# Half-wise norms: the second half's column sums closed on VectorE straight behind the last residual, ahead of the first half's second chunk

## The chip, the cores and the metric

The kernel runs on one core of a Trainium2 chip. The metric is the device time of one execution in microseconds (us); lower is better. Several runs of one kernel are given by their median. A profile shows one further execution: its span is counted from the first to the last instruction.

## The reference

The program computes two transformer blocks one after the other on 512 tokens with 1024 features, in float32. The first block has a recurrent mixer layer (HGRN2 and retention heads) and a sparse-attention layer, each followed by a SwiGLU feed-forward part and with RMS norms. The second block has an attention layer and a convolution layer, each followed by an MLP with a squared ReLU, modulated by a condition vector. What the change touches are the norms at five places: the final RMS norm of the first block and the four layer norms of the second.

```python
def rms_norm(x, g):
    xf = x.astype(jnp.float32)
    return (xf * lax.rsqrt(jnp.mean(xf * xf, axis=-1, keepdims=True) + EPS) * g).astype(x.dtype)

def layer_norm(x, g, b):
    xf = x.astype(jnp.float32)
    mu = jnp.mean(xf, axis=-1, keepdims=True)
    var = jnp.mean(jnp.square(xf - mu), axis=-1, keepdims=True)
    return ((xf - mu) * lax.rsqrt(var + EPS) * g + b).astype(x.dtype)
...
        x = layer_norm(DEEPNORM_ALPHA * x + g1 * y, ln_g[l, 0], ln_b[l, 0])
        h = modulate(x, sh2, sc2)
        x = layer_norm(DEEPNORM_ALPHA * x + g2 * sq_relu_mlp(h, mlp_w1[l], mlp_w2[l]), ln_g[l, 1], ln_b[l, 1])
```

## The kernel before

**Layout.** Features lie on the 128 partitions: the residual x is 8 tiles of 128 features by 512 tokens. Every product is made in three matmuls, because each operand is split into a high part (rounded, made by ScalarE) and a low part (the difference, made by VectorE, and in the norms by GpSimd): high by high, high by low, low by high. Weights stream in units of 128x1024, two to a pair, through `w_raw`, `w_hi` and `w_lo`. TensorE (PE) works through these units from start to end, and the other engines prepare what it reads. Every engine's order of instructions is written out by hand, and counting semaphores tie them together; an engine takes its instructions strictly in the order written.

**The five half-wise norms.** Five products end in a norm whose result the next product reads: `ffn1_down2` (called with r = 4, an RMS norm, the start of the attention stage behind it), `out2` (r = 5), `mlp0_down3` (r = 6), `out3` (r = 7) and `mlp1_down3` (r = 8, the end of the program). On each engine the end of such a product stands in a function `close_halves`, and the start of the product behind it in `open_halves`. They split the 512 tokens into two halves of 256 columns. TensorE finishes features 6 and 7 (slots s = 0 and 1) for half 0, then for half 1, so that the norm of half 0 proceeds while TensorE still multiplies for half 1.

**What the norm does, by name.** On VectorE:
- `take(half, s)` adds a finished product to x (L2063 for r = 4, L2065 else) and, for r > 4, subtracts a rough mean into `norm_xc` (L2071).
- `close(half)` adds the last tile to the sums over features: L2083 adds the last `norm_xc` tile to s1 (r > 4 only), and L2087 adds the last square to s2. GpSimd has made the sums up to there (L523, L529); ScalarE makes the squares (`square`, L1123).
- `variance(half)` (L2096 to L2099, r > 4), then ScalarE's root (L1134), then `scale(half)`: the reciprocal (L2105) and a diagonal matrix `norm_diag` (L2108).
- `centre(half, c)` (L2120, r > 4) and `normal(half, c)` (L2129 for r = 4, L2133 else) make chunk c of a half, two features of eight. There are four chunks to a half.

On TensorE `sum_half(r, half)` sums s1 and s2 over partitions (L2483 for the mean, L2477 for the columns of sums) and `spread_half` spreads the scale over partitions (L2492). On ScalarE `chunk(half, c)` modulates a chunk (L1144, two instructions) and rounds it to `h_hi` (L1152; in the last norm L1148 writes x instead). GpSimd's `low_halves` makes `h_lo` from both (L538). The next product's matmuls (L2467) wait for each chunk's `h_lo`.

The orders around the change are these. ScalarE:

```python
square(1, 0)
...
chunk(0, 0)
square(1, 1)
...
chunk(0, 1)
...
chunk(0, 2)
root_half(1)
```

TensorE's `open_halves` begins with `sum_half(r, 1)`, then multiplies chunk 0 for both slots and chunk 1 for slot 0, then does `spread_half(r, 1)`, then the rest of half 0 (five groups of six matmuls), then half 1, chunk by chunk, twelve matmuls each.

Of the kernel before, what the change touches and what calls it, by code (L numbers as in the profile page):

```python
# [171 lines left out]
def program(nc, dram, out):  # L172
    with ExitStack() as ctx:
# [242 lines left out]
        def half_cols(half):  # L416
            return slice(T // 2 * half, T // 2 * half + T // 2)

        def half_count(r, half):

            return 2 * r - 3 + half

        def halves_before(r, half, step):

            return step * (2 * (r - 4) + half)

        def centred_before(r, half, step):

            return step * (2 * (r - 5) + half)

        def stat_half(half):
            return psum[2 + 4 * half]
# [958 lines left out]
        def _(dve):  # L1391
# [631 lines left out]
            def gated_residual(name, part, r=None):  # L2023

                def body(i, s, m):
                    dve.wait_ge(unit_done, 2 * i + s + 1)
                    xm = x[:, bass.ds(m, 1), :]
                    dve.scalar_tensor_tensor(xm, row(psum[s]), mod[:, bass.ds(8 * part + m, 1), 0], xm,  # L2028
                                             ALU.mult, ALU.add).then_inc(bank_free[s], 1)
                    if r:  # L2030
                        dve.wait_ge(bank_free[s], i + 1)
                        dve.wait_ge(shift_done, r - 4)
                        dve.scalar_tensor_tensor(N["xc"][:, bass.ds(m, 1), :], row(psum[3]), -1.0 / P, xm,  # L2033
                                                 ALU.mult, ALU.add).then_inc(xc_done, 1)
                if r:
                    pairs(name, body, 0, PAIRS[name] - 2)
                    close_halves(name, part, r, body)
                else:
                    pairs(name, body)
                    dve.wait_ge(bank_free[1], PAIR0[name] + PAIRS[name])  # L2040

            def close_halves(name, part, r, body):
# [4 lines left out]
                def take(half, s):  # L2047

                    cols, m = half_cols(half), 6 + s
                    xm = x[:, m, cols]  # L2050
                    if half == 0:
                        dve.wait_ge(unit_half, 2 * (r - 4) + s + 1)
                        if r == 4:
                            ins = dve.tensor_tensor(xm, xm, psum[s][:, cols], ALU.add)
                        else:
                            ins = dve.scalar_tensor_tensor(xm, psum[s][:, cols], mod[:, 8 * part + m, 0:1], xm, ALU.mult,
                                                           ALU.add)
                        ins.then_inc(bank_free[s], 1)
                        dve.wait_ge(bank_free[s], i + 1)
                    else:  # L2060
                        dve.wait_ge(unit_done, 2 * i + s + 1)
                        if r == 4:
                            ins = dve.tensor_tensor(xm, xm, psum[6 + s][:, cols], ALU.add)  # L2063
                        else:
                            ins = dve.scalar_tensor_tensor(xm, psum[6 + s][:, cols], mod[:, 8 * part + m, 0:1], xm,  # L2065
                                                           ALU.mult, ALU.add)
                        ins.then_inc(x_half, 1)
                        dve.wait_ge(x_half, 2 * (r - 4) + s + 1)
                    if r == 4:
                        return  # L2070
                    dve.scalar_tensor_tensor(N["xc"][:, m, cols], psum[3][:, cols], -1.0 / P, xm, ALU.mult, ALU.add)\  # L2071
                       .then_inc(xc_half, 1)

                def close(half):

                    cols, last = half_cols(half), KT - 1
                    if r == 4:
                        dve.wait_ge(acc_done, 5 + half)
                    else:
                        acc = 6 + centred_before(r, half, 2)  # L2080
                        dve.wait_ge(acc_done, acc + 1)
                        dve.wait_ge(xc_half, centred_before(r, half, 2) + 2)
                        dve.tensor_tensor(N["s1"][:, cols], N["s1"][:, cols], N["xc"][:, last, cols], ALU.add)\  # L2083
                           .then_inc(s1_done, 1)
                        dve.wait_ge(acc_done, acc + 2)
                    dve.wait_ge(sq_half, halves_before(r, half, 2) + 2)
                    dve.tensor_tensor(N["s2"][:, cols], N["s2"][:, cols], N["sq"][:, last, cols], ALU.add)\  # L2087
                       .then_inc(s2_done, 1)
# [21 lines left out]
                def both(ap):  # L2110
                    return row(ap[:, 0:T // 2]).broadcast_to([P, 2, T // 2])

                def centre(half, c):

                    if r == 4:
                        return
                    if c == 0:
                        dve.wait_ge(mean_done, centred_before(r, half, 1) + 1)
                    xc = N["xc"][:, 2 * c:2 * c + 2, half_cols(half)]
                    dve.scalar_tensor_tensor(xc, both(mean_half(half)), -1.0 / D, xc, ALU.mult, ALU.add)\  # L2120
                       .then_inc(centred, 1)

                def normal(half, c):

                    if c == 0:
                        dve.wait_ge(scale_done, half_count(r, half))
                    cols, two = half_cols(half), slice(2 * c, 2 * c + 2)
                    if r == 4:
                        dve.tensor_tensor(N["xc"][:, two, cols], x[:, two, cols], both(stat_half(half)), ALU.mult)\  # L2129
                           .then_inc(y_done, 1)  # L2130
                        return
                    dve.wait_ge(centred, centred_before(r, half, 4) + c + 1)
                    dve.tensor_tensor(N["y"][:, two, cols], N["xc"][:, two, cols], both(stat_half(half)), ALU.mult)\  # L2133
                       .then_inc(y_done, 1)
# [18 lines left out]
                normal(0, 0)  # L2153
                centre(0, 1)
                take(1, 1)
                normal(0, 1)
                close(1)
                centre(0, 2)
                normal(0, 2)
                variance(1)  # L2160
# [14 lines left out]

            pairs("ffn1_down2", add_residual, 0, 2)
            close_halves("ffn1_down2", None, 4, add_residual)
            dve.wait_ge(ctx_in, 16)
            for k in range(KT):
# [975 lines left out]
```

## Time and profile before

| | us |
|---|---|
| median of 3 runs | 2628.8 |
| lowest and highest | 2627.44 and 2631.59 |
| the profiled execution's own time | 2632.85 |
| its span | 2631.0 |

In that span TensorE is busy for 2562.0 us, VectorE for 1581.0, ScalarE for 1048.3 and GpSimd for 258.3. Since TensorE is nearly always busy, what a local change is worth is read at the places where TensorE stands still. A row of the timeline gives the start in us, the duration in us, the engine, the line of the kernel, the operation, what it writes and reads, the shape, how many instructions are merged in the row, and in brackets how long the engine was idle before and who released it. An instruction's duration includes the time that it is held up after its start.

### The profile page before, as it was taken

How to read it: one execution, taken by the hardware profiler on the slowest of the kernel's cores; microseconds unless marked ns; L12 is line 12 of the kernel's file. 1: busy time of each engine (PE TensorE's matmuls, PEld its weight loads, DVE VectorE, ACT ScalarE, POOL GpSimd, SP SyncE). 2: the span in 40 equal slices, each digit the busy share in tenths (PEclk: the TensorE clock that was granted, in tenths of full speed). 3: DMA queues.
4: the chain of work that ended last, by engine and by line, in shares of the span. 5: the costliest groups of instructions: out<-in, count | busy, mean ns of one | idle time of the engine just before them, and what ended most of it. 6: DMA issues, size and time to landing. Idle time of an engine off the chain costs nothing.

```text
span 2631.0 us, 37917 instructions
## 1 busy us (share of the span) xinstructions
PE 2562.0 (97%) x13134; PEld 2109.1 (80%) x13134; DVE 1581.0 (60%) x2460; ACT 1048.3 (40%) x1663; POOL 258.3 (10%) x187
## 2 busy tenths in 40 slices
PE   8999999999999999999989999999999999999997
PEld 6887788888887878888878776788888888888886
DVE  6764665656578866565665786555555665644445
ACT  5334522223357852222353266553223422522333
POOL 2320100000320010000030100310000401300002
PEclk9999999999999999999999999999999999999999
DMA  3221344444320034444432100234444243332322
GB/s 133 73 88 65 119 137 144 144 145 149 135 73 26 26 112 143 144 143 144 144 120 72 41 1 1 80 112 144 144 144 143 95 145 114 104 102 96 96 96 80
DMA packets 79338, 277.48 MB, mean 105 GB/s; under 512 B 8448, under 2 KB 11904, under 8 KB 78720
## 3 DMA queue, kind: packets, MB, share of 16 engines
q1 hardware_dynamic: 58560, 205.55, 23.9%
q10 hardware_dynamic: 20672, 70.51, 8.2%
q8 instruction: 68, 1.11, 0.2%
q14 instruction: 38, 0.31, 0.0%
HBM read 273.92 MB, written 2.10 MB: 105 GB/s over the span
## 4 chain that ended last, share of the span: by engine, by line
PE 86%; DVE 7%; ACT 3%; issue 1%; DMA 1%; POOL 1%; ACTq 0%; DVEq 0%; SPq 0%; POOLq 0%
PE banks L2423 64%; PE banks L2564 5%; PE banks L2993 2%; PE banks L2467 2%; PE banks L2829 2%; DVE w_lo L1403 1%; PE banks L2935 1%; PE banks L2867 1%; PE banks L2844 1%; PE banks L2598 1%; DMA w_raw<-weights 1%; PE banks L2947 1%; ACT w_hi L679 1%; PE banks L2964 1%; DVE ada_raw L1426 0%
## 5 line engine op out<-in xcount | busy, mean ns | idle before, releaser
L679 ACT ACTIVATE w_hi<-w_raw 128x1024 fp32r<-128x1024 f32 x367 | 386.4, 1053 | 621.7 <-PE banks L2423 515.1
L2423 PE MATMUL banks<-h_hi,w_hi 128*128 128x512 f32 x1600 | 628.0, 392 | 1.1 <-DVE w_lo L1403 0.7
L2423 PE MATMUL banks<-h_hi,w_lo 128*128 128x512 f32 x1600 | 623.1, 389 | 0.0
L2423 PE MATMUL banks<-h_lo,w_hi 128*128 128x512 f32 x1600 | 622.9, 389 | 0.0
L1403 DVE TENSOR_TENSOR w_lo<-w_raw,w_hi 128x1024 fp32r<-128x1024 f32 x367 | 474.1, 1292 | 108.7 <-ACT w_hi L679 91.9
L2423 PE MATMUL banks<-g_hi,w_hi 128*128 128x512 f32 (+1 forms) x1108 | 427.5, 386 | 9.9 <-DVE w_lo L1403 8.8
L2423 PE MATMUL banks<-g_hi,w_lo 128*128 128x512 f32 (+1 forms) x1108 | 423.6, 382 | 0.0
L2423 PE MATMUL banks<-g_lo,w_hi 128*128 128x512 f32 (+1 forms) x1108 | 423.6, 382 | 0.0
L2423 PEld LDWEIGHTS banks<-h_hi,w_hi 128*128 128x128 f32 x1600 | 300.4, 188 | 66.8 <-issue 2.8
L2423 PEld LDWEIGHTS banks<-h_lo,w_hi 128*128 128x128 f32 x1600 | 300.5, 188 | 62.7 <-issue 1.7
L2423 PEld LDWEIGHTS banks<-h_hi,w_lo 128*128 128x128 f32 x1600 | 300.4, 188 | 62.8
L2423 PEld LDWEIGHTS banks<-g_hi,w_hi 128*128 128x128 f32 x1108 | 208.7, 188 | 58.8 <-DVE w_lo L1403 14.8
L2423 PEld LDWEIGHTS banks<-g_lo,w_hi 128*128 128x128 f32 x1108 | 208.8, 188 | 40.6 <-issue 1.0
L2423 PEld LDWEIGHTS banks<-g_hi,w_lo 128*128 128x128 f32 x1108 | 208.6, 188 | 40.5
L2028 DVE SCALAR_TENSOR_TENSOR x<-banks,mod,x 128x512 f32 (+1 forms) x72 | 53.9, 749 | 163.4 <-PE banks L2423 163.2
L1426 DVE CUSTOM_DVE_ANT_0 ada_raw<-ada_raw,rows_c 128x1024 f32<-128x1024 f32 x112 | 138.6, 1238 | 0.0
L2336 DVE TENSOR_TENSOR ffn_hid<-ffn_act 128x512 f32<-128x512 f32 x64 | 44.3, 692 | 131.9 <-ACT ffn_act L1347 131.9
L2564 PE MATMUL banks<-h_hi,w_hi 128*128 128x512 f32 x256 | 104.5, 408 | 10.3 <-DVE w_lo L1403 10.3
L1347 ACT ACTIVATE ffn_act<-banks 128x512 f32<-128x512 f32 x64 | 38.3, 598 | 189.1 <-PE banks L2423 184.2
L523 POOL TENSOR_TENSOR norm_s<-norm_xc 128x512 f32<-128x512 f32 x4 | 8.8, 2198 | 952.6 <-DVE norm_xc L2033 952.6
L2564 PE MATMUL banks<-h_hi,w_lo 128*128 128x512 f32 x256 | 101.1, 395 | 0.0
L2564 PE MATMUL banks<-h_lo,w_hi 128*128 128x512 f32 x256 | 101.1, 395 | 0.0
(409 smaller groups left out, 3304.5 us busy)
## 6 DMA issues: line engine op xcount, KB each, us to landing
w_raw<-weights SPq DMA_DIRECT2D x384, 512.0 KB, 3.3
ada_raw<-ada ACTq DMA_DIRECT2D x112, 512.0 KB, 3.3
nsa_bias<-nsa_bias ACTq DMA_DIRECT2D x6, 512.0 KB, 3.7
x<-x SPq DMA_DIRECT2D x4, 512.0 KB, 6.9
out<-x SPq DMA_DIRECT2D x8, 256.0 KB, 2.1
mix_cum<-ret_tab ACTq DMA_DIRECT2D x1, 1024.0 KB, 4.8
rows_c<-c_rows ACTq DMA_DIRECT2D x1, 1024.0 KB, 5.5
nsa_w<-cmp_w ACTq DMA_DIRECT2D x1, 1024.0 KB, 5.5
```

The lines of the kernel that those rows point to most:

```text
L679: act.activation(w_hi[s][:], w_raw[s][:], ACT.Copy).then_inc(w_hi_done, 1)
L1347: act.activation(F["act"][:, s, :], psum[s], ACT.Relu).then_inc(bank_free[s], 1)
L1403: dve.tensor_tensor(w_lo[s][:], w_raw[s][:], w_hi[s][:].bitcast(F32), ALU.subtract)\
L1426: dve.tensor_tensor_reduce(ada_raw[:], ada_raw[:], c_row[:, who, :], 1.0, 0.0, ALU.mult, ALU.add, ada_col[:]).then_inc(ada_done, 1)
L2028: dve.scalar_tensor_tensor(xm, row(psum[s]), mod[:, bass.ds(8 * part + m, 1), 0], xm, ALU.mult, ALU.add).then_inc(bank_free[s], 1)
L2336: dve.tensor_tensor(F["hid"][:, s, :], F["act"][:, s, :], F["act"][:, s, :], ALU.mult)\
L2423: mm = pe.matmul(bank, w[s][:, k, :], m[:, k, :], start=(n == 0 and a == 0), stop=(n == kts - 1 and a == 2))
L2467: mm = pe.matmul(bank[:, cols], w[slot][:, k, :], m[:, k, cols], start=(k == 0 and a == 0), stop=(k == kts - 1 and a == 2))
L2564: mm = pe.matmul(bank, w[s][:, k, :], m[:, k, :], start=(k == 0 and a == 0), stop=(k == KT - 1 and a == 2))
L2598: mm = pe.matmul(grams[:, cols(t)], left[:, h, cols(t)], right[:, h, cols(t)], start=True, stop=True)
L2829: mm = pe.matmul(banks[:, 4 - 2 * (j % 2) + b, 0:W], S["qs"][:, h, qi * P:(qi + 1) * P], S["ks"][:, b, part, m // 4, 0:W], start=(part == ...
L2993: mm = pe.matmul(banks[:, 2 + 2 * b + a, 0:c1 - c0], q, keys[:, c0:c1], start=True, stop=True)
```

## The change

In VectorE's `close_halves`, the call `close(1)` moves up by one line: from behind `normal(0, 1)` to ahead of it. It holds for all five norms.

```diff
@@ -2153,8 +2153,8 @@
                 normal(0, 0)
                 centre(0, 1)
                 take(1, 1)
+                close(1)
                 normal(0, 1)
-                close(1)
                 centre(0, 2)
                 normal(0, 2)
                 variance(1)
```

On VectorE, at the end of `ffn1_down2` (r = 4), the order changes as follows; `norm_s_68` is s2, `norm_xc` is where this norm puts its normalized chunk, and a row that ends in x2 or x3 stands for as many equal instructions.

```order
 L2063 TENSOR_TENSOR x<-x,banks 128x256 [waits unit_done]
-L2129 TENSOR_TENSOR norm_xc<-x,banks 128x2x256 [waits x_half]
-L2087 TENSOR_TENSOR norm_s_68<-norm_s_68,norm_sq 128x256 [waits sq_half,acc_done]
-L2129 TENSOR_TENSOR norm_xc<-x,banks 128x2x256 x2
+L2087 TENSOR_TENSOR norm_s_68<-norm_s_68,norm_sq 128x256 [waits sq_half,acc_done,x_half]
+L2129 TENSOR_TENSOR norm_xc<-x,banks 128x2x256 x3
 L2105 RECIPROCAL norm_r<-norm_r 128x2 [waits root_done]
```

The one sum, which waits for ScalarE's square (`sq_half`), now stands ahead of the chunk that filled that wait.

On VectorE, at the end of `out2` (r = 5), the order changes as follows, and in the same way for r = 6, 7 and 8; `norm_s_73` is s1.

```order
 L2065 SCALAR_TENSOR_TENSOR x<-banks,mod,x 128x256 [waits unit_done]
 L2071 SCALAR_TENSOR_TENSOR norm_xc<-banks,x 128x256 [waits x_half]
-L2133 TENSOR_TENSOR norm_y<-norm_xc,banks 128x2x256 [waits centred]
 L2083 TENSOR_TENSOR norm_s_73<-norm_s_73,norm_xc 128x256 [waits xc_half,acc_done]
 L2087 TENSOR_TENSOR norm_s_68<-norm_s_68,norm_sq 128x256 [waits sq_half,acc_done]
+L2133 TENSOR_TENSOR norm_y<-norm_xc,banks 128x2x256 [waits centred]
 L2120 SCALAR_TENSOR_TENSOR norm_xc<-banks,norm_xc 128x2x256
 L2133 TENSOR_TENSOR norm_y<-norm_xc,banks 128x2x256 [waits centred]
```

The first L2133 row, chunk 1 of half 0, goes behind the two sums. No instruction is added or removed, and the other engines' orders stay as they are.

## Rows read from the trace of the kernel before

**Rows 1.** Page, part 1: busy us (share of the span) and instructions.

```profile
PE 2562.0 (97%) x13134; PEld 2109.1 (80%) x13134; DVE 1581.0 (60%) x2460; ACT 1048.3 (40%) x1663; POOL 258.3 (10%) x187
```

**Rows 2.** Waits of PE, 2060 to 2130 (around r = 6): total us, times, longest us.

```profile
PE banks L2483 <- DVE norm_s L2083: 3.2, 2, 2.9
PE banks L2467 <- POOL h_lo L538: 1.1, 2, 0.8
```

**Rows 3.** Timeline around the sums of half 1 in out2, all engines.

```profile
1705.07 0.42 DVE L2071 SCALAR_TENSOR_TENSOR norm_xc<-banks,x 128x256 f32<-128x256 f32 x1
1705.41 0.68 DVE L2133 TENSOR_TENSOR norm_y<-norm_xc,banks 128x512 f32<-128x512 f32 x1
1705.58 0.40 ACT L1123 ACTIVATE norm_sq<-norm_xc 128x256 f32<-128x256 f32 x1
1705.75 1.26 POOL L538 TENSOR_TENSOR h_lo<-norm_sq,h_hi 128x512 fp32r<-128x512 f32 x1 [1.05 <-ACT h_hi L1152]
1706.00 1.29 DVE L2083 TENSOR_TENSOR norm_s<-norm_s,norm_xc 128x256 f32<-128x256 f32 x1
1707.21 0.41 DVE L2087 TENSOR_TENSOR norm_s<-norm_s,norm_sq 128x256 f32<-128x256 f32 x1
1707.44 0.67 PE L2483 MATMUL banks<-norm_s,tab 128*128 128x256 f32 x2 [2.93 <-DVE norm_s L2083]
1707.55 0.68 DVE L2120 SCALAR_TENSOR_TENSOR norm_xc<-banks,norm_xc 128x512 f32<-128x512 f32 x1
1708.26 0.69 DVE L2133 TENSOR_TENSOR norm_y<-norm_xc,banks 128x512 f32<-128x512 f32 x1
1708.99 1.09 ACT L1144 ACTIVATE norm_sq<-norm_y,aux,ln_cols 128x256 f32<-128x256 f32 x2 [1.11 <-DVE norm_y L2133]
```

**Rows 4.** Timeline of out2 further on: root, diagonal, spread, chunks of half 1.

```profile
1710.65 0.28 ACT L1134 ACTIVATE norm_r<-norm_st,tab 128x2 f32<-128x2 f32 x1
1711.16 1.22 DVE L2108 TENSOR_TENSOR norm_diag<-tab,norm_r 128x256 f32<-128x256 f32 x1
1712.49 0.64 PE L2492 MATMUL banks<-norm_diag,tab 128*128 128x256 f32 x2
1713.17 0.69 DVE L2133 TENSOR_TENSOR norm_y<-norm_xc,banks 128x512 f32<-128x512 f32 x1 [0.19 <-PE banks L2492]
1717.51 0.39 PE L2467 MATMUL banks<-h_hi,w_hi 128*128 128x256 f32 x1 [0.82 <-POOL h_lo L538]
```

**Rows 5.** Timeline of ffn1_down2 (r = 4), the same place.

```profile
1349.39 0.40 ACT L1123 ACTIVATE norm_sq<-x 128x256 f32<-128x256 f32 x1
1349.56 1.27 POOL L538 TENSOR_TENSOR h_lo<-norm_sq,h_hi 128x512 fp32r<-128x512 f32 x1 [3.23 <-ACT h_hi L1152]
1349.89 1.22 DVE L2087 TENSOR_TENSOR norm_s<-norm_s,norm_sq 128x256 f32<-128x256 f32 x1 [0.63 <-ACT norm_sq L1123]
1351.74 1.09 ACT L1144 ACTIVATE norm_sq<-norm_xc,mod,ln_cols 128x256 f32<-128x256 f32 x2 [0.30 <-DVE norm_xc L2129]
1353.88 1.26 DVE L2108 TENSOR_TENSOR norm_diag<-tab,norm_r 128x256 f32<-128x256 f32 x1
1356.09 1.05 PE L2492 MATMUL banks<-norm_diag,tab 128*128 128x256 f32 x2
```

**Rows 6.** Timeline of mlp1_down3 (r = 8), the same place.

```profile
2616.17 0.68 DVE L2133 TENSOR_TENSOR norm_y<-norm_xc,banks 128x512 f32<-128x512 f32 x1
2616.29 0.42 ACT L1123 ACTIVATE norm_sq<-norm_xc 128x256 f32<-128x256 f32 x1 [1.88 <-DVE norm_xc L2071]
2616.76 0.42 DVE L2083 TENSOR_TENSOR norm_s<-norm_s,norm_xc 128x256 f32<-128x256 f32 x1
2617.43 0.68 DVE L2120 SCALAR_TENSOR_TENSOR norm_xc<-banks,norm_xc 128x512 f32<-128x512 f32 x1
```

**Rows 7.** Windows of PE in out2: us, busy us (matmuls), granted clock, DMA.

```profile
1709.00:1712.00 3.00, 3.00 (x16) 0.50 0.00 0
1713.00:1716.00 3.00, 3.00 (x27) 1.00 0.00 0
```

## The prediction

> **What bounds the kernel now.** I read the page's busy times first, then TensorE's waits, then the timeline of each of the five norms. The reader should see three things. TensorE is busy for 97% of the span [rows 1], so a local change counts only where TensorE stands still or where its matmuls wait for a chunk. Behind `out2` it stands still twice: 2.93 us until the sum L2483, released by VectorE's L2083, and later 0.82 us for GpSimd's `h_lo` [rows 3, 4]. The waits around r = 6 show the same two [rows 2] (3.2 us in two waits, since the first half's sum waits a little too), and the view reads alike for r = 7, so one reading serves three norms. The long wait invites the change, since s1 and s2 come sooner if they stand further up. But a wait that is shortened is worth something only if the same engine does not wait later for something that has not moved.
>
> So I followed the 0.82 us back. The matmuls of half 1 wait for `h_lo` of half 1, chunk 0. That comes from `normal(1, 0)` at 1713.17, which stands behind the spread (1712.49) and the diagonal (1711.16), behind the root at 1710.65 [rows 4]. ScalarE does the root only after chunk (0, 2), which began at 1708.99 after ScalarE had been idle for 1.11 us until VectorE's L2133 of 1708.26 [rows 3]. From a chunk's start to the root is 1710.65 - 1708.99 = 1.66 us, and that is what one ScalarE chunk costs. The sums are in this chain only because chunk 2 stands behind them on VectorE. What counts is when VectorE gives ScalarE chunks 1 and 2, not when the sums are done.
>
> **The change, part by part.** It adds and removes nothing, and no DMA moves. L2083 and L2087 go ahead of one L2133, in r = 4 only L2087. Queued behind them on VectorE are now chunks 1 and 2 of half 0, and ScalarE waits for these.
>
> *r = 5, 6, 7.* Before: L2133 starts at 1705.41, ScalarE takes chunk 1 right behind its 0.68 us, and VectorE's L2083 is held up meanwhile: it takes 1.29 us [rows 3] where the same instruction takes 0.42 with GpSimd quiet [rows 6]. GpSimd's `h_lo` ran from 1705.75 to 1707.01, and VectorE's next instruction starts at 1707.21, 0.20 after that end.
> After: L2071 ends at 1705.49. A wait for another instruction's end costs about 0.1 (in r = 4 the square ends at 1349.79 and L2087 starts at 1349.89 [rows 5]), so L2083 runs from 1705.60 to 1706.02. That is before GpSimd's `h_lo` asks (1705.75), so GpSimd goes second: about 1705.9 to 1707.2. L2087 needs ScalarE's square, which ends at 1705.98, and the same 0.1: ready at 1706.08. By then GpSimd is at work, and L2087 is held until 1707.2, the next instruction starting 0.20 later, at 1707.4. Only now L2133 for chunk 1 runs, 0.69, to 1708.09; ScalarE starts chunk 1 0.04 later, at 1708.13, instead of at about 1706.13. Chunk 2 follows 1.66 later, at 1709.79 instead of 1708.99, since ScalarE's idle 1.11 us absorbed the rest. The root, the diagonal, the spread and all of half 1 are 0.80 later. The diagonal keeps its long 1.22 us [rows 4], a hold-up like L2083's, since it and the `h_lo` that holds it both hang on chunk 2. TensorE's gain, s1 sooner by 1.4 us and s2 by 0.1, ends in a longer wait for the spread. The cost is 0.80 each, 2.40 in all.
>
> The bounds for one of these norms: if L2087 slips in before GpSimd, VectorE goes on at 1706.08 + 0.34 = 1706.42 (0.34 is from L2087's start to the next instruction's, 1707.21 to 1707.55) and chunk 2 starts 0.98 earlier than above, a gain of 0.18. If L2083 too is caught by GpSimd, it ends as before and L2087 ends at 1707.62, so L2133 starts at 1707.55: a loss of 0.95. I take 0.80, since the VectorE sums and diagonals of this size that meet a GpSimd instruction (1.29, 1.22, 1.22, 1.26) all show a full hold-up [rows 3 to 5].
>
> The Trainium skill, "SBUF — State Buffer", section "SBUF: two separate sides", says that an instruction of VectorE with two SBUF inputs and one of GpSimd exclude each other for the whole instruction. [...]
>
> *r = 4.* L2087 has no use for its new place: it waited 0.63 us for ScalarE's square already and started at 1349.89 [rows 5]. The square stands behind ScalarE's chunk 0, which doesn't move. So the sum comes no earlier, while chunk 1 comes behind L2087, held by GpSimd (1.22 us): L2129 starts 0.20 behind GpSimd's end of 1350.83, at 1351.03, ScalarE has chunk 1 at 1351.03 + 0.69 + 0.04 = 1351.76 and chunk 2 at 1353.42 instead of 1351.74, so the root and the diagonal are 1.68 later. The diagonal ended at 1355.14 and now ends at 1356.82. TensorE did not need it before 1356.09 [rows 5]; it now waits until about 1356.9. Slack of 0.95 is eaten, and 0.8 is left as a loss.
>
> *r = 8.* ScalarE makes no `h_lo` input here and GpSimd is quiet, so nothing is held. But two waits are now uncovered. Before, L2133 filled them and L2120 started at 2617.43. After, the square ends at 2616.71 and L2087 starts at 2616.81; L2133 follows 0.34 later and L2120 another 0.59 behind it (as L2083 behind L2133, 2616.17 to 2616.76), at 2617.74 [rows 6]. That is 0.3 later, and all behind it is VectorE's own chain. The bounds are 0, if some of it is made up by a wait for TensorE's sums that comes sooner, and 0.5.
>
> The sum: 3 x 0.80 + 0.8 + 0.3 = 3.5 us. Against the profiled execution (2632.85, span 2631.0) that gives 2636.4. That execution lies 4.05 above the median of the runs, so the forecast for a median is 2628.8 + 3.5 = 2632.3 us.
>
> **The rivals.** *Clock.* After the 2.93 us of idleness TensorE falls to its lower level, 1.2 GHz, from 1709 to 1712 at least (14 matmuls start in 3 us, 0.214 each), and is back at 2.4 GHz from 1713 on (25 start in 3 us, 0.12 each) [rows 7]; their counts hold two begun before. It comes back just before the spread, which took 0.64; in r = 4 it took 1.05 [rows 4, 5]. The new order cuts one long idle time into several: until s1, until s2, for chunk 1's `h_lo` (about 0.6 us) and for the spread (up to 1.2 us). If the clock is still low at the spread, 0.4 to 0.5 comes on top, and if it stays low into half 1, twelve matmuls of a chunk take 12 x 0.214 = 2.57 us against ScalarE's pitch of 1.66, 0.9 more per chunk. With one such chunk and the spread in each of four norms that is 4 x 1.4 = 5.6 more: 2637.9. It decides from the point where the lower level lasts beyond the spread. For it speaks that the low level lasted 3 us and more although TensorE multiplied without a break; against it, that the first idle time is shorter than before. It is slower by over 0.2%.
> *The sums slip through.* L2087 runs before GpSimd in r = 5 to 7 (the bound above): -3 x 0.18 + 0.8 + 0.3 = +0.6, 2629.4. Against it: GpSimd has been waiting since 1705.75, ahead of L2087's 1706.08.
> *TensorE decides after all.* With s1 at 1706.0 the clock may never fall, and the 14 matmuls of [rows 7] would take 0.12 us each instead of 0.214: 1.3 us per norm, 2628.8 - 3.9 + 1.1 = 2626.0, or less with the few low ones outside that window. It needs TensorE to be what ends the stage; the 0.82 us for `h_lo` speaks against it. The Trainium skill, "TensorE: Matmul & The Clock Gate", section "Why this matters for your kernels", advises against idle gaps between bursts of matmuls, because the clock then drops; by that advice a shorter gap is a gain, and the rows agree only as far as the clock itself goes.
> That the change would not do what it says is the case in r = 4, and is in the forecast.
>
> **How the numbers follow.** A measurement of this kernel can tell about 0.2%, 5.3 us, from no change. Forecast 0.60 (of itself 2.5 to 5 us more, nearly all within 0.2%), clock 0.24, slipping through 0.10, TensorE decides 0.06. Faster by over 0.2%: 0.03, half of the last. Slower by over 0.2%: 0.20 from the clock and 0.04 from the forecast's upper edge, 0.24. Within: the remaining 0.73. The range reaches from below the slipping case to the clock case: 2628.0 to 2637.5.
>
> **What would show it.** In the new profile L2083 in `out2` should take about 0.42 and start 0.1 behind L2071; L2087 should be the long one (about 1.2 us), in r = 4 as before; ScalarE's idle time should stand before chunk 1 and not before chunk 2; the root should come 5.96 us after L2071's end instead of 5.16; TensorE's 2.93 us should become about 1.5 and a new wait should stand at L2492. The forecast is wrong if the end of half 1's chunks, counted from L2071, comes no later than before, if L2492 is reached without a wait, or if the clock stays low in half 1.

## The result, and the profile after

The changed kernel took 2634.62 us (median of 14 runs, 2631.74 to 2638.57) against 2627.99 us for the kernel before (14 runs, 2624.25 to 2635.58): a ratio of 1.0021, with a 95% interval of 1.0013 to 1.0028. By the ratio that is 5.5 us slower, between 3.4 and 7.4; the two medians alone lie 6.6 us apart. The forecast was 3.5 us more, or 2632.3 us, so the direction held, the time lies in the range of 2628.0 to 2637.5, and the size was at the interval's lower end. The profiled execution has a span of 2636.8 us, 5.8 more than before.

TensorE's waits around r = 6, which answer to [rows 2] (total us, times, longest us):

```profile
PE banks L2483 <- DVE norm_s L2083: 1.9, 2, 1.7
PE banks L2467 <- POOL h_lo L538: 1.8, 2, 1.6
PE banks L2492 <- DVE norm_diag L2108: 1.0, 1, 1.0
PE banks L2477 <- DVE norm_s L2087: 0.3, 1, 0.3
```

The long wait for s1 fell from 2.93 to 1.66 us. In its place stand a wait for s2 (0.3), one for chunk 1's `h_lo` (1.6) and one for the diagonal (1.0). Two kinds of wait have become four, and together they are longer (5.0 us against 4.3). In `out2` TensorE waits only for s1 (1.66), s2 (0.31) and the diagonal (0.28) and is never idle behind the spread: its matmuls run at the lower clock from 1709.3 to 1719.5 there and arrive later.

The timeline of `out2` in the changed kernel answers to [rows 3] and [rows 4]. The columns are as there.

```profile
1707.30 0.42 DVE L2071 SCALAR_TENSOR_TENSOR norm_xc<-banks,x 128x256 f32<-128x256 f32 x1
1707.81 0.40 ACT L1123 ACTIVATE norm_sq<-norm_xc 128x256 f32<-128x256 f32 x1
1707.83 0.43 DVE L2083 TENSOR_TENSOR norm_s<-norm_s,norm_xc 128x256 f32<-128x256 f32 x1
1707.98 1.40 POOL L538 TENSOR_TENSOR h_lo<-norm_sq,h_hi 128x512 fp32r<-128x512 f32 x1 [1.05 <-ACT h_hi L1152]
1708.32 1.35 DVE L2087 TENSOR_TENSOR norm_s<-norm_s,norm_sq 128x256 f32<-128x256 f32 x1
1708.40 0.67 PE L2483 MATMUL banks<-norm_s,tab 128*128 128x256 f32 x2 [1.66 <-DVE norm_s L2083]
1709.59 0.68 DVE L2133 TENSOR_TENSOR norm_y<-norm_xc,banks 128x512 f32<-128x512 f32 x1
1710.30 1.10 ACT L1144 ACTIVATE norm_sq<-norm_y,aux,ln_cols 128x256 f32<-128x256 f32 x2 [2.09 <-DVE norm_y L2133]
...
1713.61 0.28 ACT L1134 ACTIVATE norm_r<-norm_st,tab 128x2 f32<-128x2 f32 x1
1714.12 1.23 DVE L2108 TENSOR_TENSOR norm_diag<-tab,norm_r 128x256 f32<-128x256 f32 x1
1715.41 1.22 PE L2492 MATMUL banks<-norm_diag,tab 128*128 128x256 f32 x2 [0.28 <-DVE norm_diag L2108]
```

L2083 is short now (0.43) and L2087 is the one that GpSimd holds (1.35). ScalarE stands idle for 2.09 us ahead of chunk 1, where it stood 1.11 ahead of chunk 2. The root comes 5.89 us behind the end of the last residual (1707.72), where it was 5.16. The spread takes 1.22 us where it took 0.64, since TensorE is at its lower clock (1.2 GHz). The window row of TensorE (us, busy us, granted clock, DMA share, GB/s) answers to [rows 7]:

```profile
1713.00:1716.00 3.00, 2.72 (x11) 0.50 0.00 0
```

In this table each mark is counted from the end of the last residual (L2071, for r = 4 L2063), in us. The last column is the end of the last matmul of half 1, the moment from which TensorE runs on without the norm.

| norm | root before | root after | spread takes, before | after | half 1 ends, before | after |
|---|---|---|---|---|---|---|
| r = 4 | 4.86 | 6.49 | 1.05 | 1.22 | 19.18 | 20.07 |
| r = 5 | 5.16 | 5.89 | 0.64 | 1.22 | 18.69 | 19.97 |
| r = 6 | 5.16 | 5.88 | 0.65 | 1.22 | 18.71 | 19.94 |
| r = 7 | 5.16 | 5.88 | 0.65 | 0.70 | 18.72 | 19.41 |
| r = 8 | 3.30 | 3.60 | 1.22 | 1.22 | (VectorE's chain) | +0.30 |

The differences are 0.89, 1.28, 1.23, 0.69 and 0.30: 4.4 us. The rest of the 5.8 us between the two spans lies where nothing was altered: 0.3 before the first of these norms and 1.0 between r = 4 and r = 5. Of that 1.0, 0.8 arises between 1496 and 1521, where the lower clock lasted longer: from 1500 to 1512 TensorE's mean granted clock was 0.57, and 0.72 before.

### The profile page after: what moved, and what is told of

Same layout as the page of the kernel before. It is cut to its first block, busy times and chain, and to the rows that moved or that the text cites. A ratio compares the mean times of both kernels' runs of the same rounds, so it can differ in the third digit from the quotient of the medians.

```text
span 2636.8 us, 37917 instructions
## 1 busy us (share of the span) xinstructions
PE 2567.9 (97%) x13134; PEld 2113.2 (80%) x13134; DVE 1582.2 (60%) x2460; ACT 1047.6 (40%) x1663; POOL 258.6 (10%) x187
## 3 DMA queue, kind: packets, MB, share of 16 engines
q8 instruction: 68, 1.11, 0.2%
## 4 chain that ended last, share of the span: by engine, by line
PE 86%; DVE 7%; ACT 4%; issue 1%; DMA 1%; POOL 1%; ACTq 0%; DVEq 0%; SPq 0%; POOLq 0%
PE banks L2423 64%; PE banks L2564 5%; PE banks L2993 3%; PE banks L2467 2%; PE banks L2829 2%; DVE w_lo L1403 1%; PE banks L2935 1%; PE banks L2867 1%; PE banks L2844 1%; PE banks L2598 1%; DMA w_raw<-weights 1%; ACT w_hi L679 1%; PE banks L2947 1%; PE banks L2964 1%; ACT norm_sq L1144 0%
```

## The experiments

**Three questions.** Is the loss made by the order, that is, by L2087 held by GpSimd ahead of ScalarE's chunks? What is the clock's part? And why is the measured loss above the forecast? In what follows "residual" stands for the end of the last L2071 (L2063 for r = 4), from which marks are counted.

**The hold-up alone.** GpSimd's first `h_lo` waits until s2 is closed; the order on VectorE is the changed one.

```diff
                         pool.wait_ge(y_hi, 4 * KT + halves_before(r, half, 4) + c + 1)
+                        if half == 0 and c == 0:
+                            pool.wait_ge(s2_done, half_count(r, 1))
```

> The changed kernel, but GpSimd starts the first h_lo of half 0 only when VectorE has closed s2, so that L2087 meets no GpSimd instruction (r = 4 to 7). Order theory with the hold-up as its cause: L2087 takes 0.42 instead of 1.35, chunk 2 on ScalarE starts 3.3 to 3.4 us behind the residual in r = 5 to 7 (changed kernel 4.24, before 3.50) and about 4.1 in r = 4 (4.84, before 3.20); half 1 ends at 18.5 to 18.7 in r = 5 to 7, about 19.4 in r = 4. Total against before -0.3 to +0.6 us, ratio 0.9999 to 1.0002. Rival (the order costs even without the hold-up, or the late h_lo of chunk 0 costs as much): the ratio stays at 1.0015 to 1.002.

Measured: ratio 0.9997 (0.9988 to 1.0006). The timeline in `out2` (this kernel's lines are shifted by two: L2085 and L2089 are the sums, L2135 is chunk 1, L540 `h_lo`):

```profile
1702.20 0.42 DVE L2085 TENSOR_TENSOR norm_s<-norm_s,norm_xc 128x256 f32<-128x256 f32 x1
1702.68 0.43 DVE L2089 TENSOR_TENSOR norm_s<-norm_s,norm_sq 128x256 f32<-128x256 f32 x1
1703.02 0.68 DVE L2135 TENSOR_TENSOR norm_y<-norm_xc,banks 128x512 f32<-128x512 f32 x1
1703.25 1.27 POOL L540 TENSOR_TENSOR h_lo<-norm_sq,h_hi 128x512 fp32r<-128x512 f32 x1 [1.94 <-DVE norm_s L2089]
1703.73 1.09 ACT L1146 ACTIVATE norm_sq<-norm_y,aux,ln_cols 128x256 f32<-128x256 f32 x2 [1.16 <-DVE norm_y L2135]
```

With GpSimd out of the way L2089 takes 0.43 us, ScalarE waits 1.16 instead of 2.09, the root stands at 4.95 and half 1 ends at 18.49, 18.49 and 18.50 in r = 5 to 7, 0.2 below the kernel before. The order by itself costs nothing there. What costs is one instruction of VectorE held for 0.93 us ahead of the chunks. The rival, a loss without the hold-up, falls in these three norms. In r = 4 it does not. Counted from L2087's start (the next run shows why), half 1 of r = 4 ended at 17.41, against 18.18 with the hold-up and 16.58 to 16.73 in the order of before, all with the clock high at the spread. So there the hold-up is half of the loss. The other half stays when GpSimd is out of the way, and chunk 1 then stands behind a sum that itself waits 0.86 us for its square. The expectation of 19.4 for r = 4 was 1.1 too high: ScalarE stood 0.5 earlier relative to the residual, and the clock was high. In r = 8, where GpSimd is quiet, the 0.30 stayed.

**Only r = 4 changed.**

```diff
                 take(1, 1)
+                if r == 4:
+                    close(1)
                 normal(0, 1)
-                close(1)
+                if r > 4:
+                    close(1)
```

> The sums move ahead only in r = 4; r = 5 to 8 keep the order of before. Order theory: in r = 4 chunk 2 on ScalarE starts 4.8 us behind the end of the last residual (before 3.20), TensorE waits about 0.9 us for the spread and the last matmul of half 1 ends 20.0 +- 0.1 behind the residual (before 19.2); r = 5 to 7 end at 18.7 and r = 8 has its root at 3.30, as before. Total +0.8 to +0.9 us. Rival (the clock alone makes the loss): r = 4 ends at 19.2 to 19.4 wherever TensorE's level is the same as before, whatever ScalarE's chunks do.

One run, 2631.45 us, which says nothing of so small a difference, and its profile: half 1 of r = 4 ended at 20.19 and chunk 2 started at 4.97. TensorE waited 0.27 us ahead of the spread, not the 0.9 expected. The last residual came 0.15 earlier relative to ScalarE here, so I count r = 4 from L2087's start, which ScalarE's square sets in every version: before 17.83, the changed kernel 18.71, this one 18.69. The clock is low at the spread in all three, so the loss of 0.88 is the order's: the spread starts 0.73 later in the changed kernel and 0.72 here, and takes 1.22 us instead of 1.05 now that TensorE stands idle ahead of it. r = 6, 7 and 8 were as before, but r = 5, whose order is that of before, ended at 19.97 instead of 18.69. Its sums ran at the lower clock (L2486 and L2480 are the sums there, L2495 the spread):

```profile
1704.74 1.19 PE L2486 MATMUL banks<-norm_s,tab 128*128 128x256 f32 x2 [2.93 <-DVE norm_s L2083]
1705.72 1.71 PE L2480 MATMUL banks<-tab,norm_s 128*128 128x1 f32 x8
1709.65 0.42 DVE L2108 TENSOR_TENSOR norm_diag<-tab,norm_r 128x256 f32<-128x256 f32 x1
1711.11 0.60 PE L2495 MATMUL banks<-norm_diag,tab 128*128 128x256 f32 x2
```

They took 1.19 and 1.71 us where they took 0.67 and 0.95 before (granted clock 0.50 from 1704.7 to 1707.5; 1.00 at the same place before). The variance and the diagonal came later too, but they did not set the end: the diagonal was done at 1710.07, and TensorE, busy without a pause since its sums, reached the spread only at 1711.11. Here TensorE decided, and an unaltered norm lost 1.3 us. So where the low clock falls in a norm is worth as much as the change, and it is not fixed by the program. A single profile can't price a norm without a look at its clock.

**The changed kernel again**, unaltered.

> The changed kernel once more, unaltered. In its first profile half 1 ended 20.0, 19.9 and 19.4 us behind the last residual in r = 5, 6, 7, with the spread at 1.22, 1.22 and 0.70. Order theory: the marks of ScalarE and VectorE repeat within 0.05 (chunk 2 at 4.24, root at 5.88), and each of r = 5 to 7 ends at 19.4 where the spread takes 0.70 and at 19.9 to 20.0 where it takes 1.22; which of them has which is free to differ from the first profile. Ratio 1.0013 to 1.0028. Rival (the low clock belongs to a place in the program): the same two norms have 1.22 again.

Measured: 2637.27 us (9 runs), ratio 1.0024 (1.0014 to 1.0034). Half 1 ended at 19.95, 19.94 and 19.43 in r = 5 to 7, chunk 2 started at 4.23 or 4.24 and the root stood at 5.88 or 5.89: VectorE's and ScalarE's marks repeat within 0.02. r = 5 and 6 had the spread at 1.22 again and r = 7 at 0.70, as the rival had said, so two profiles can't tell a place in the program from chance. r = 4 differed: its spread took 0.70.

```profile
1347.53 1.19 DVE L2087 TENSOR_TENSOR norm_s<-norm_s,norm_sq 128x256 f32<-128x256 f32 x1 [0.90 <-ACT norm_sq L1123]
1354.44 0.70 PE L2492 MATMUL banks<-norm_diag,tab 128*128 128x256 f32 x2 [0.89 <-DVE norm_diag L2108]
```

**The changed kernel with the clock held up.** Filler matmuls go into a bank that nothing reads, 6 ahead of half 1's sums and 4 ahead of its spread.

```diff
                 pe.wait_ge(w_lo_done, 2 * p0 + 1)
+                filler(6)
                 sum_half(r, 1)
...
                 steps(0, 0, 1)
+                filler(4)
                 spread_half(r, 1)
```

Each filler is `pe.matmul(psum[5], w_hi[1][:, 0, :], w_hi[1][:, 0:4, :]...)`, 512 columns.

> The changed kernel with filler matmuls (128x512, high part of a weight by itself, into a bank that nothing reads): 6 ahead of half 1's sums and 4 ahead of its spread, in TensorE's idle time there, for r = 4 to 7. Nothing else is altered. Theory (order 0.7 to 0.8 per norm plus 0.5 where the clock is low at the spread): the clock stays at its upper level, the spread takes 0.70 in every norm, half 1 ends at 19.4 in r = 5 to 7, ratio 1.0007 to 1.0015 of before. Rival (the order costs nothing and the clock all): ratio 0.999 to 1.0003.

Measured: ratio 1.0016 (1.0007 to 1.0025), the point a little above what was expected. The spread took 0.70 in all four norms, for example in `out2`:

```profile
1705.28 0.28 ACT L1134 ACTIVATE norm_r<-norm_st,tab 128x2 f32<-128x2 f32 x1
1705.94 1.08 PE L2527 MATMUL banks<-w_hi 128*128 128x512 f32 x4
1707.07 0.70 PE L2492 MATMUL banks<-norm_diag,tab 128*128 128x256 f32 x2
```

Half 1 ended at 19.44, 19.44 and 19.45. So with the clock up the order costs 0.7 per norm in r = 5 to 7, and the low clock at the spread adds the other 0.5 (1.22 - 0.70). By the marks the filler takes part of the loss back, not all; the time alone doesn't tell this version from the changed kernel (1.0016 against 1.0021 and 1.0024, with overlapping intervals). The rival, that the clock is everything, falls: its upper end of 1.0003 lies below the interval. Set beside the run without the hold-up, which had the same order and the spread at 0.70 or 0.71 in these norms too, half 1 ends 0.95 later, so the gain of that run was the hold-up's and not the clock's.

**The kernel before with the clock held up**: the same filler, 10 ahead of the sums, none ahead of the spread.

> The kernel before with 10 filler matmuls ahead of half 1's sums (about 2.2 of the 2.93 us in which TensorE is idle), r = 4 to 7. If ScalarE's and GpSimd's chunks decide the end of the norm, TensorE's matmuls start half 0 at the upper level and only wait longer: half 1 ends at 18.7 in r = 5 to 7 as before, up to 1 us less in r = 4 where the matmuls limit the spread; ratio 0.9995 to 1.0001. Rival (TensorE decides after all): each norm ends 1.3 us sooner, -4 to -5 us, ratio 0.998 to 0.9985.

Measured: ratio 0.9992 (0.9983 to 1.0001). The point lies below the expected 0.9995, and the interval touches the rival's 0.9985, so it is the marks that decide. Half 1 ended at 18.73, 18.73 and 18.72 in r = 5 to 7, within 0.04 of where the low clock had it. TensorE's matmuls of half 0 ran at 2.4 GHz, and it only waited longer, for the diagonal:

```profile
1703.31 0.70 PE L2483 MATMUL banks<-norm_s,tab 128*128 128x256 f32 x2 [0.59 <-DVE norm_s L2083]
1708.38 0.70 PE L2492 MATMUL banks<-norm_diag,tab 128*128 128x256 f32 x2 [1.35 <-DVE norm_diag L2108]
```

That refutes the third rival of the prediction for r = 5 to 7: a faster TensorE gains nothing there. But it has no slack to lose either. In the kernel before it reached the spread at 7.00 without a wait, 0.11 behind the end of the diagonal (6.89), and r = 5 of the run with only r = 4 changed shows that a slower TensorE costs 1.3. In r = 4 its speed does decide. Counted from L2087, half 1 ended at 17.83 before, with TensorE at its lower clock, and here at 16.60.

**s1 alone ahead** (r = 5 to 8), s2 behind chunk 1.

```diff
                 take(1, 1)
+                if r > 4:
+                    close(1, 1)
                 normal(0, 1)
-                close(1)
+                close(1, 2)
```

> Only L2083 (s1) goes ahead of chunk 1, for r = 5 to 8; L2087 (s2) stays behind chunk 1, and r = 4 is as before. Order theory: L2083 takes 0.42, no GpSimd in flight; chunk 1 is 0.5 later than before, L2087 is held by GpSimd and ends about 0.1 sooner, so chunk 2 starts 3.3 to 3.5 us behind the residual (before 3.50) and half 1 ends at 18.5 to 18.7: no loss, ratio 0.9995 to 1.0002 of before. Rival (any sum ahead of chunk 1 costs what it delays chunk 1): half 1 ends 0.4 to 0.5 later in three norms, +1.5 us, ratio 1.0006.

Measured: ratio 0.9997 (0.9989 to 1.0006). Chunk 2 started at 3.30 or 3.31 and half 1 ended at 18.51 and 18.50 in r = 5 and 6, and at 19.02 in r = 7, with the spread at 1.22. In `out2` (L2091 is s2, L2124 the centring of chunk 2):

```profile
1702.40 0.90 DVE L2091 TENSOR_TENSOR norm_s<-norm_s,norm_sq 128x256 f32<-128x256 f32 x1
1703.22 0.68 DVE L2124 SCALAR_TENSOR_TENSOR norm_xc<-banks,norm_xc 128x512 f32<-128x512 f32 x1
```

Half of what the change does is harmless: s1 meets no GpSimd instruction where it stands now. The loss is s2's. Behind chunk 1 it is held for a shorter time (0.90 us instead of 1.35), and most of that is covered by ScalarE's work on the chunk: ScalarE waits 0.38 us ahead of chunk 2.

**s2 in GpSimd's gap.** For r = 5 to 7, s1 ahead of chunk 1 and s2 behind the centring of chunk 2, when GpSimd has ended one `h_lo` and not begun the next.

```diff
                 take(1, 1)
+                if 4 < r < 8:
+                    close(1, 1)
                 normal(0, 1)
-                close(1)
-                centre(0, 2)
+                if 4 < r < 8:
+                    centre(0, 2)
+                    close(1, 2)
+                else:
+                    close(1)
+                    centre(0, 2)
```

> For r = 5 to 7 L2083 goes ahead of chunk 1 and L2087 behind the centring of chunk 2, in the gap between two of GpSimd's h_lo instructions; r = 4 and 8 as before. Order theory: L2087 takes 0.42 instead of 1.2 to 1.35, chunk 2 starts on ScalarE at 2.8 to 2.9 us behind the residual (before 3.50), root at 4.5 (before 5.16); the spread is then limited by TensorE's 18 low-clock matmuls, half 1 ends 0.3 to 0.7 sooner per norm, -0.9 to -2 us, ratio 0.9993 to 0.9997. Rival (the sums' own time decides): no gain, since s2 is not done sooner than before.

Measured: 2629.16 us against 2631.11 for the kernel before, measured beside it, ratio 0.9989 (0.998 to 0.9998): faster than the kernel before by an interval that just leaves out 1, and below the 0.9993 expected. In r = 6 (L2085 s1, L2137 chunk 1, L2124 the centring, L2091 s2, L2102 the subtraction in the variance):

```profile
2065.36 0.42 DVE L2085 TENSOR_TENSOR norm_s<-norm_s,norm_xc 128x256 f32<-128x256 f32 x1
2065.51 1.41 POOL L538 TENSOR_TENSOR h_lo<-norm_sq,h_hi 128x512 fp32r<-128x512 f32 x1 [1.04 <-ACT h_hi L1152]
2065.70 0.68 DVE L2137 TENSOR_TENSOR norm_y<-norm_xc,banks 128x512 f32<-128x512 f32 x1
2066.30 0.68 DVE L2124 SCALAR_TENSOR_TENSOR norm_xc<-banks,norm_xc 128x512 f32<-128x512 f32 x1
2066.90 0.42 DVE L2091 TENSOR_TENSOR norm_s<-norm_s,norm_sq 128x256 f32<-128x256 f32 x1
2068.41 1.15 DVE L2102 TENSOR_TENSOR norm_st<-norm_st 128x2 f32<-128x2 f32 x1
```

L2137 and L2124, which read one operand from PSUM, run at full speed while GpSimd works, and s2 takes 0.42. Half 1 ended at 18.15, 18.17 and 18.16, which is 0.55 sooner per norm, 1.6 us in all; the ratio's point says 2.9 and its interval 0.5 to 5.3. The rival, that only the moment of s2 counts, falls: s2 is closed at 2.07 behind the residual, hardly sooner than the 2.13 of before.

The last row shows what is still lost. The variance now comes so early that L2102, on 128x2 elements, meets GpSimd's next `h_lo` (2068.26 to 2069.55) and takes 1.15 us instead of 0.16. Chunk 3 queues behind it on VectorE, and the reciprocal behind chunk 3, so that the root, started at 4.54 and done at 4.84, is taken up only at 5.74. With s1 alone ahead the row before it was caught in the same way (0.92 us). In this version VectorE's own chain decides, not ScalarE's.

**The same with filler**, 6 ahead of the sums (r = 4 to 7) and 4 ahead of the spread (r = 5 to 7).

> The version with s1 ahead of chunk 1 and s2 in the gap of GpSimd (ratio 0.9989), with 6 filler matmuls ahead of half 1's sums and 4 ahead of the spread (none there in r = 4). Half 1 ended at 18.15 to 18.17 there with the spread at 0.70 in all three norms, so the filler has nothing to win in that state: 18.15 again, r = 4 up to 1 us less, ratio 0.9983 to 0.999. If filler delays the sums or the spread, half 1 ends later than 18.3.

Measured: ratio 0.999 (0.998 to 0.9999). Half 1 ended at 18.17 in all three norms, and r = 4 at 16.58 behind L2087 instead of 17.83. The filler gained nothing in r = 5 to 7 that the profile shows, and the two ratios don't tell the versions apart. Beside the kernel before with filler (18.73), which also has the clock high, the new order ends 0.56 sooner: the gain is the order's.

## Why the prediction was right, point by point

**Where the end of a norm is decided.** Right. ScalarE's chunks and the root behind them set it: the root moved by 0.73 and half 1 by 0.69 where the clock was the same (r = 7), and making TensorE faster in the kernel before moved nothing there. Two limits showed: TensorE stood level with the diagonal, so that a slower TensorE took over (19.97 in r = 5 of the run with only r = 4 changed), and in the versions with the two sums apart VectorE's chain did.

**The cost in r = 5 to 7**, forecast 0.80 each. The mechanism was right and the size a little high: L2083 started 0.11 behind L2071 and took 0.43, L2087 took 1.35, chunk 1 started at 2.58 (forecast 2.64), chunk 2 at 4.25 (4.30), the root at 5.89 (5.96). One reading of the rows was off: s1 comes 1.27 us sooner by them (1707.29 to 1706.02), not 1.4, and TensorE's wait became 1.66, not 1.5; nothing in the sum hangs on it. With the clock at its upper level at the spread the cost is 0.69 to 0.72. The bound "slips in before GpSimd" was what the run without the hold-up built, and its gain came out as 0.2 against the 0.18 worked out.

**The clock.** Given 0.24 as a rival, and at nothing in the sum; a part of it came. The spread took 1.22 instead of 0.64 in two norms of three, in both profiles of the changed kernel, which is 0.5 to 0.6 each. The larger part, twelve low matmuls of a chunk in half 1, did not: from the spread to the end of half 1 there was 12.28 us in r = 5, where the kernel before had 11.69, and the difference is the spread's own. The low level did last beyond the spread there, as the rival had asked (granted clock 0.50 from 1716.6 to 1719.5), but it fell on the rest of half 0. TensorE reached half 1 at 13.64 without a wait, where it waited 0.82 us at that place before, so its slack absorbed the slow matmuls. The rival's own sum, 2637.9, lies 0.4 above the range that was said to reach to it.

**r = 4**, forecast 0.8. Right for a TensorE at its lower clock (0.88), and there by luck as far as the first profile again had the low clock in this norm. Here stands the term that was mis-sized. The forecast took the slack of 0.95 us, TensorE not needing the diagonal before 1356.09, from a profile in which its 18 matmuls ran at 1.2 GHz. Counted from L2087 to the end of half 1, the runs showed:

| r = 4, us from L2087 | order of before | s2 ahead of chunk 1 | the same without the hold-up |
|---|---|---|---|
| clock low at the spread | 17.83, 17.83 | 18.71, 18.69 | not measured |
| clock high at the spread | 16.73, 16.60, 16.58 | 18.18, 18.19 | 17.41 |

With the clock high there is little slack, and the order costs 1.45 to 1.6 us, of which the hold-up is 0.77. Seen the other way, the order of before turns a high clock into 1.1 to 1.25 us, and the changed one into 0.5.

**r = 8**, forecast 0.3: measured 0.30.

**The sum.** The forecast was 3.5 us. The marks of the two first profiles give 4.4: 0.9 for r = 4, 3.2 for r = 5 to 7 with two low spreads, 0.3. With r = 4 at the high clock it would be about 5. The ratio gives 5.5, with an interval of 3.4 to 7.4 that holds all of these. Whether anything beyond the marks is in it stays open. What lies between 3.5 and 4.4 is the low clock at two spreads, 1.0 to 1.2 us, which the sum had left out, less the 0.1 that it had too high in each of three norms.

**The rival "the sums slip through"** did not occur by itself: in r = 4 to 7 of both profiles of the changed kernel, and of the one with filler, GpSimd's `h_lo` started ahead of L2087, which took 1.18 to 1.35 us.

## What to carry to other kernels

Ahead of moving an instruction up, ask what it will meet there: in these traces an instruction of VectorE with two SBUF operands that began while GpSimd's `h_lo` ran was held for GpSimd's whole remainder (L2087 1.35 us instead of 0.42, and even the 128x2 one 1.15 instead of 0.16), and one that reads an operand from PSUM was not held at all (chunk 1 and the centring of chunk 2, 0.68 us each). Put the first kind into GpSimd's gaps and fill its running time with the second kind. And a wait of the busiest engine is not yet a loss; follow its next wait back first, since what is released earlier is worth nothing if the same engine stands again for something that now comes later.

## What the runs showed of the hardware that was not expected

The place of TensorE's low clock differs between executions of the same order. The sums of `out2` in the order of before took 0.67 and 0.95 us in one profile and 1.19 and 1.71 in another, which, with the order unchanged in that norm, moved its end by 1.3 us. In the kernel before with filler, r = 8, where neither the order nor the filler differs from before, had its mean's sum at 0.96 us instead of 0.70 and its root at 4.28 instead of 3.30.

GpSimd is held up a little as well: in the changed kernel its `h_lo` of half 0, chunk 0 started at 1707.98, while L2083 ran until 1708.26, and took 1.40 us instead of 1.26. The 0.14 is half of the 0.28 that the two overlap; that GpSimd too waits for the other's whole remainder is not shown.
